# Tiles of a two-layer hybrid backbone at other SBUF addresses, with the order of all work kept

## The chip, the cores and the metric

The kernel runs on one core of one Trainium2 chip. The metric is device time in microseconds of one execution; the times shown are single executions and their median.

## What is computed

The reference is a backbone of two layers over 256 context and 256 latent tokens of width 1024. Each layer is a SwiGLU FFN, a token mixer and a second SwiGLU FFN, each after an RMSNorm with a shift, a scale and a gate made from the conditioning vectors. The mixer of layer 0 is a state-space scan (S5), that of layer 1 a gated DeltaNet.

```python
def swiglu(h, w13, w2):
    a, b = jnp.split(h @ w13, 2, axis=-1)
    return (jax.nn.silu(a) * b) @ w2
...
for i in range(DEPTH):
    mx = (silu(c) @ mod_w[i] + mod_b[i]).reshape(bsz, N_MOD, 1, D_MODEL)
    x = x + 0.5 * mx[:, 2] * swiglu(ada_norm(x, norm_g[i, 0], mx[:, 0], mx[:, 1]), ffn_w13[i, 0], ffn_w2[i, 0])
...
    hx = ada_norm(x, norm_g[i, 1], mx[:, 3], mx[:, 4])
...
    x = x + mx[:, 5] * ox
    x = x + 0.5 * mx[:, 8] * swiglu(ada_norm(x, norm_g[i, 2], mx[:, 6], mx[:, 7]), ffn_w13[i, 1], ffn_w2[i, 1])
return rms_norm(x, final_g)
```

## The kernel before

**Layout and stages.** Activations lie with the channel on the partitions: x is 8 tiles of 128 partitions x 512 tokens in float32. The program runs straight through: the modulation vectors, norm, FFN 0, norm, S5 and its gated linear unit, norm, FFN 1, norm, FFN 2, norm, DeltaNet and its output projection, norm, FFN 3, final norm. FFN 3 and the output projection work on the 256 latent tokens alone. An FFN goes over its 22 inner tiles in three parts of 8, 8 and 6; each part has an up phase and a down phase.

**Matmuls of three.** Every large matrix product is done as three float32r matmuls: weights and activations are both split into a high and a low part, and high x high, high x low and low x high are added in PSUM. `mm3` (lines 219 to 221) does this for one output tile, `mm3_pair` (line 228) for two. The activation parts are hh and hl in the up phases, the GLU and the DeltaNet projections, hidh and hidl in the down phases, and yh and yl in the output projection. The weight parts are whi and wlo.

**Weights.** A block is 1 MB of weights in one of two slots of raw. SyncE loads it in two halves (`load_halves`, line 237), ScalarE copies each half to whi (`split_hi`, line 254), VectorE subtracts to get wlo (`split_lo`, line 260), and TensorE reads 48 weight tiles of 128 x 128 from a full block. Each step waits on a semaphore of its half and slot.

**Other lines that are spoken of.** ScalarE's SiLU (line 495) and VectorE's product (line 522) fill gt; GpSimd makes hidh (line 573) and hidl (line 575) from it; VectorE adds the down projection to x (line 558). A norm squares x on GpSimd (line 348), takes the reciprocal on VectorE (line 366), scales x into tmp (line 373) and makes hh (line 324) and hl (line 384). Line 592 has the modulation matmuls, which read cvec, and line 1430 writes gwal, at the beginning of the DeltaNet stage.

**Queues and order.** The order of each engine's work is written out in the program, with semaphores alone between the engines. Loads of weights go through SyncE's queue. No instruction depends on an address.

**SBUF.** Tiles are given addresses one after another in the order in which they are declared. A tile that is declared in a stack that has been closed gives its bytes back, so that later tiles lie over it; such overlays hold the FFN's tiles (hidh, hidl, modw, rows, cb, junk, gt, hh, hl), those of the S5 tables and scan, and those of the DeltaNet, each beginning at byte 99,200 of a partition. The first tile, x, begins at byte 16,512. With the sizes in the program this gives, in bytes of one partition:

| tile | bytes | begins before | past a multiple of 2048 |
|---|---|---|---|
| x | 16,384 | 16,512 | 128 |
| raw | 16,384 | 32,896 | 128 |
| whi | 16,384 | 49,280 | 128 |
| wlo | 16,384 | 65,664 | 128 |
| consts | 6,144 | 82,048 | 128 |
| mods, gs, hg | 1,920 | 88,192 | 128 |
| rstd | 2,048 | 90,336 | 224 |
| gwal | 1,024 | 97,152 | 896 |
| cvec | 1,024 | 98,176 | 1,920 |
| hidh | 16,384 | 99,200 | 896 |
| hidl | 16,384 | 115,584 | 896 |
| modw | 16,384 | 131,968 | 896 |
| gt | 4,096 | 192,384 | 1,920 |
| hh | 16,384 | 196,480 | 1,920 |
| hl | 16,384 | 212,864 | 1,920 |
| yh (DeltaNet) | 9,216 | 179,040 | 864 |

One row of hh, hidh or x for a tile of channels is 2,048 bytes (512 tokens); the latent tokens are its second 1,024 bytes. A weight tile is 512 bytes, four of them 2,048. A row of yh is 1,024 bytes.

Of the kernel before, what the change touches and what calls it, by code (L numbers as in the profile page):

```python
# [14 lines left out]
F32 = mybir.dt.float32  # L15
# [4 lines left out]
P = 128  # L20
D = 1024
KT = D // P
# [6 lines left out]
NMOD = 9  # L29
# [94 lines left out]
def program(nc, A, out):  # L124

    ctx = ExitStack()
    with ctx:
# [6 lines left out]
        def sb(name, shape, dt=F32, stack=None):  # L134
            return (stack or ctx).enter_context(nc.sbuf_tensor(name, shape, dt))


        x = sb("x", [P, KT, T])
        raw = sb("raw", [P, 2, BLK])
        whi = sb("whi", [P, 2, BLK], F32R)  # L140
        wlo = sb("wlo", [P, 2, BLK], F32R)
        consts = sb("consts", [P, len(CONSTS), P])
        mods = sb("mods", [P, 2, NMOD * KT, 2])
        gs = sb("gs", [P, 2, 3, KT, 2])
        hg = sb("hg", [P, 2, 3, KT, 2])
        ng = sb("ng", [P, 2, 3, KT])
        fg = sb("fg", [P, KT])
        rstd = sb("rstd", [P, T])
# [7 lines left out]
        early.close()  # L156
        gwa = sb("gwa", [P, KT, 4 * H])
        gwah = sb("gwah", [P, KT, 4 * H], F32R)
        gwal = sb("gwal", [P, KT, 4 * H], F32R)
        cvec = sb("cvec", [P, KT, 32])  # L160
        PS = ctx.enter_context(nc.psum_tensor("PS", [P, 8, 512], F32))

        def const(name):
# [1 line left out]


        ffn = ExitStack()
        hidh = sb("hidh", [P, PARTS[0][1], T], F32R, ffn)
        hidl = sb("hidl", [P, PARTS[0][1], T], F32R, ffn)
        modw = sb("modw", [P, MS, 4 * 512], F32, ffn)  # L170
        rows = sb("rows", [P, 512], F32, ffn)
        cb = sb("cb", [P, 2, D], F32, ffn)
# [4 lines left out]
        hl = sb("hl", [P, KT, T], F32R, ffn)  # L177
        ffn.close()
        nrm = ExitStack()
        tmp = sb("tmp", [P, KT, T], F32, nrm)  # L180
        nrm.close()

# [466 lines left out]
                    dve.tensor_scalar(hg[:, layer, n, :, :], one, 1.0 if n == 1 else 0.5, None, ALU.mult).then_inc(mods_ready, 1)  # L649

        prs = ExitStack()
        sb("hid_at", [P, 6144], F32, prs)
        ep = sb("ep", [P, 2, 6, 64], F32, prs)
        sb("ep_end", [P, 256], F32, prs)
# [16 lines left out]
        t4 = sb("t4", [P, GPB * (L + 1) * C16], F32, prs)  # L671
        prs.close()
        ups = ExitStack()
        sb("to_hh", [P, 24320], F32, ups)
        v = sb("v", [P, 24, 64], F32, ups)
        s5p = sb("s5p", [P, 3, 64], F32, ups)
# [9 lines left out]
        yd = nc.dram_tensor("yd", (D, T), F32, kind="Internal").ap()  # L686

        s5st = ExitStack()
        U = sb("U", [P, G, NK], F32, s5st)
        hS = sb("hS", [P, KT, L, NK], F32, s5st)  # L690
        vwS = sb("vwS", [P, 2, 2, 8, P], F32, s5st)
# [396 lines left out]
        def s5_sp(sp):  # L1088
# [5 lines left out]
            for part_, (k0, k1) in enumerate(S5_PARTS):  # L1094
# [5 lines left out]
                for st in range(L):  # L1100
                    src = bass.AP(hd.tensor, hd.offset + k0 * P * T + st * NK, [[T, C16], [C16 * T, 8 * (k1 - k0)], [1, NK]])
                    sp.dma_start(U[C16 * st:C16 * st + C16, 8 * k0:8 * k1, :], src).then_inc(u_in[part_], 16)
                if part_ == 0:
# [15 lines left out]
        def scan_order(t, d):  # L1119

            return t if d == 0 else t.rearrange("p (a j) -> p a j", a=2)[:, :, ::-1]

        def s5_pe(pe):
            def inputs(b):
# [5 lines left out]
                for gd in range(8):  # L1130
                    for r in range(2):
                        for g2 in range(2):
                            g = 8 * b + 2 * (gd // 2) + g2
                            last = pe.matmul(PS[64 * g2:64 * g2 + 64, 2 * s + r, gd * NK:(gd + 1) * NK],
                                             vwS[:, s, r, gd, 64 * g2:64 * g2 + 64], scan_order(U[:, g, :], gd % 2),
                                             start=True, stop=True)
                last.then_inc(V_ready, 1)

            def outputs(c):
                s = c % 2  # L1140

                def dst(pr, g2):
                    return PS[:, 4 + 2 * s + g2, pr * NK:(pr + 1) * NK]
# [5 lines left out]
                for pr in range(GPB):  # L1149
                    for g2 in range(2):  # L1150
                        gl = 2 * pr + g2
                        pe.matmul(dst(pr, g2), mS[:, s, gl, :], U[:, 8 * c + gl, :], start=pr == 0, stop=False,
                                  skip_group_check=True)
# [156 lines left out]
                    last.then_inc(blk_done[s], 1)  # L1310

        gst = ExitStack()
        pk = sb("pk", [P, 2, CTX + 4], F32, gst)
        pv = sb("pv", [P, 2, CTX + 4], F32, gst)
        pq = sb("pq", [P, 1, LAT + 4], F32, gst)
# [823 lines left out]
```

## Time and profile before

| | |
|---|---|
| three runs | 2404.7, 2392.39, 2399.65 us |
| median | 2399.65 us |
| profiled execution, its own time | 2398.18 us |
| its span, first to last instruction | 2396.4 us |
| busy share, TensorE, VectorE, ScalarE, GpSimd | 89%, 67%, 29%, 32% |
| chain that ended last: matmuls of line 228 | 36.2% of the span |
| chain that ended last: matmuls of lines 219 to 221 | 15.8% of the span |

The busy share is the part of the span in which an engine had an instruction of the program running. Matmuls overlap in the pipeline, so what one costs in a steady run is read from the distance of their starts, not from their durations. The chain that ended last is followed back from the last instruction, at each step to what released it. The granted clock is the share of TensorE's full clock: 1.00 is 2.4 GHz and 0.50 is 1.2 GHz.

### The profile page before, as it was taken

To read this page: it belongs to the slowest core of one execution; us is meant where nothing else is said; L and a number is where in the kernel's file an instruction comes from. 1 tells how busy PE (TensorE), PEld (TensorE's weight loads), DVE (VectorE), ACT (ScalarE), POOL (GpSimd) and SP (SyncE) were. 2 spreads that over 40 slices of the span, in tenths; PEclk is the share of its full clock that TensorE was granted. 3 is DMA by queue.
4 is the path that set the end of the run, shared out by engine and by line. 5 is a ranking of instruction groups with operands and counts; after the bars stand their busy time and mean duration, and the time that the engine had idled before them with its cause. 6 is when DMAs were issued, how large, how long until landed. Compare 5 with 4: busy or idle time off the path is not lost.

```text
span 2396.4 us, 34067 instructions
## 1 busy us (share of the span) xinstructions
PE 2125.8 (89%) x12486; PEld 1811.1 (76%) x12486; DVE 1609.4 (67%) x2255; ACT 704.0 (29%) x992; POOL 755.7 (32%) x588
## 2 busy tenths in 40 slices
PE   3898998972889899999899999869999999788997
PEld 0676777752878688887688888668888888778997
DVE  7966886853433886858894854637777777745555
ACT  1311221231133321212331222333434434324432
POOL 2243663742523120203320202303333322323123
PEclk6999999996679899999999999969999999988999
DMA  7354653639943344445353532210111111003553
GB/s 285 127 210 164 214 188 143 213 134 201 295 114 121 138 169 149 180 136 182 115 202 124 195 110 88 74 43 29 35 35 35 35 35 35 0 18 128 187 177 105
DMA packets 104689, 309.62 MB, mean 129 GB/s; under 512 B 27680, under 2 KB 39456, under 8 KB 95136
## 3 DMA queue, kind: packets, MB, share of 16 engines
q1 hardware_dynamic: 89392, 285.80, 35.5%
q10 hardware_dynamic: 12528, 12.33, 1.7%
q0 software_dynamic: 2688, 10.42, 1.1%
q8 instruction: 50, 0.82, 0.1%
q14 instruction: 31, 0.25, 0.0%
HBM read 280.26 MB, written 28.25 MB: 129 GB/s over the span
## 4 chain that ended last, share of the span: by engine, by line
PE 59%; issue 16%; DVE 10%; POOL 8%; DMA 2%; ACT 2%; SPq 1%; DVEq 1%; ACTq 0%; POOLq 0%
PE PS L228 36%; PE PS L219 5%; PE PS L221 5%; PE PS L220 5%; POOL EE L1883 2%; DVE wlo L260 2%; PE PS L1161 1%; POOL DTs L1873 1%; DVE t L927 1%; POOL X L1879 1%; DMA vwS<-vwd 1%; DVE bx L928 1%; PE PS L592 1%; DVE bx L926 1%; DVE rstd L366 1%
## 5 line engine op out<-in xcount | busy, mean ns | idle before, releaser
L228 PE MATMUL PS<-hh,whi 128*128 128x512 f32 (+1 forms) x1792 | 510.6, 367 | 42.9 <-DVE hl L384 32.1
L260 DVE TENSOR_TENSOR wlo<-raw,whi 128x1024 fp32r<-128x1024 f32 x328 | 488.1, 1528 | 85.7 <-ACT whi L254 82.7
L228 PE MATMUL PS<-hl,whi 128*128 128x512 f32 (+1 forms) x1792 | 506.1, 364 | 0.0
L228 PE MATMUL PS<-hh,wlo 128*128 128x512 f32 (+1 forms) x1792 | 505.3, 363 | 0.0
L254 ACT ACTIVATE whi<-raw 128x1024 fp32r<-128x1024 f32 x328 | 329.0, 1051 | 309.4 <-PE PS L221 283.2
L228 PEld LDWEIGHTS PS<-hh,whi 128*128 128x128 f32 x1792 | 323.3, 192 | 106.7 <-issue 51.4
L228 PEld LDWEIGHTS PS<-hl,whi 128*128 128x128 f32 x1792 | 325.1, 191 | 52.6
L228 PEld LDWEIGHTS PS<-hh,wlo 128*128 128x128 f32 x1792 | 324.7, 191 | 52.7
L573 POOL CAST hidh<-gt 128x512 f32 (+2 forms) x88 | 63.1, 717 | 892.4 <-DVE gt L522 892.4
L219 PE MATMUL PS<-hidh,whi 128*128 128x512 f32 (+1 forms) x704 | 262.2, 372 | 35.4 <-DVE x L558 24.2
L220 PE MATMUL PS<-hidl,whi 128*128 128x512 f32 (+1 forms) x704 | 258.9, 368 | 0.0
L221 PE MATMUL PS<-hidh,wlo 128*128 128x512 f32 (+1 forms) x704 | 258.8, 368 | 0.0
L621 DVE CUSTOM_DVE_ANT_0 junk<-modw,cb,modb 128x1024 f32<-128x1024 f32 x160 | 215.5, 1347 | 4.3
L495 ACT ACTIVATE gt<-PS 128x512 f32<-128x512 f32 (+1 forms) x88 | 47.9, 545 | 570.9 <-PE PS L228 570.8
L558 DVE SCALAR_TENSOR_TENSOR x<-PS,hg,x 128x256 f32<-128x256 f32 (+1 forms) x176 | 77.3, 478 | 188.9 <-PE PS L221 188.5
L219 PEld LDWEIGHTS PS<-hidh,whi 128*128 128x128 f32 x704 | 135.2, 192 | 62.3 <-issue 24.5
L575 POOL TENSOR_TENSOR hidl<-gt,hidh 128x512 f32 (+2 forms) x88 | 157.0, 1784 | 12.6 <-POOL hidh L573 10.8
L522 DVE TENSOR_TENSOR gt<-gt,PS 128x512 f32<-128x512 f32 (+1 forms) x88 | 54.5, 619 | 148.1 <-ACT gt L495 146.6
L221 PEld LDWEIGHTS PS<-hidh,wlo 128*128 128x128 f32 x704 | 135.1, 192 | 21.9
L220 PEld LDWEIGHTS PS<-hidl,whi 128*128 128x128 f32 x704 | 135.4, 192 | 20.7
L1872 POOL TENSOR_TENSOR DTi<-DTm,consts 128x256 f32<-128x256 f32 x16 | 17.8, 1110 | 293.3 <-ACT DTm L1665 293.3
L1680 ACT ACTIVATE BT<-PS 128x512 f32<-128x512 f32 x80 | 47.8, 597 | 152.1 <-PE PS L1560 78.4
(298 smaller groups left out, 2951.3 us busy)
## 6 DMA issues: line engine op xcount, KB each, us to landing
modw<-in_mod_w SPq DMA_DIRECT2D x72, 1024.0 KB, 4.8
raw<-in_w_gdn SPq DMA_DIRECT2D x32, 512.0 KB, 4.0
cxd<-cx POOLq DMA_DIRECT2D x16, 576.0 KB, 4.5
cxS<-cxd SPq DMA_DIRECT2D x8, 1152.0 KB, 5.9
raw<-in_w_f0p0a SPq DMA_DIRECT2D x16, 512.0 KB, 6.6
vwd<-vws ACTq DMA_DIRECT2D x16, 512.0 KB, 7.1
raw<-in_w_f0p1a SPq DMA_DIRECT2D x16, 512.0 KB, 6.5
raw<-in_w_glu SPq DMA_DIRECT2D x16, 512.0 KB, 4.0
```

What stands on the lines that cost most here:

```text
L219: pe.matmul(dst, w_h, xh, start=first, stop=False)
L220: pe.matmul(dst, w_h, xl, start=False, stop=False)
L221: return pe.matmul(dst, w_l, xh, start=False, stop=last)
L228: ended = pe.matmul(dst, of[:, slot, c:c + P], moving, start=first and part_ == 0, stop=last and part_ == 2)
L254: act.activation(whi[:, s, c], raw[:, s, c], ACT.Copy).then_inc(whi_ready[half][s], 1)
L260: dve.tensor_tensor(wlo[:, s, c], raw[:, s, c], whi[:, s, c].bitcast(F32), ALU.subtract)\
L522: dve.tensor_tensor(gt[:, s, c0:T], gt[:, s, c0:T], PS[:, 2 + s, c0:T], ALU.mult).then_inc(gt_ready[s], 1)
L558: last = dve.scalar_tensor_tensor(out=xv, in0=pv, scalar=hg[:, layer, n, bass.ds(dt, 1), w:w + 1].rearrange("p a b -> p (a b)"), in1=xv, o ...
L573: pool.tensor_copy(hidh[:, bass.ds(2 * i + s, 1), c0:T], gt[:, s:s + 1, c0:T]).then_inc(hidh_ready[s], 1)
L575: pool.tensor_tensor(hidl[:, bass.ds(2 * i + s, 1), c0:T], gt[:, s:s + 1, c0:T], hidh[:, bass.ds(2 * i + s, 1), c0:T].bitcast(F32), ALU.su ...
L621: dve.tensor_tensor_reduce(out=junk[:, :], in0=modw[:, k % MS, D * j:D * j + D], in1=cb[:, w, :], scale=1.0, scalar=modb[:, layer, a:a + 1 ...
L1883: last = pool.tensor_tensor(EE[:, d, n, :, :], NN[:, d, :, :], const(name).unsqueeze(1).to_broadcast([P, NCH, CH]), ALU.mult)
```

## The change

The tiles mods, gs and hg (1,920 bytes together) are declared ahead of x. x, raw, whi, wlo and consts begin 1,920 bytes later, and ng and all that follow keep their places. cvec is declared in a stack of its own that is closed at once, so that gwal lies over it. The FFN's tiles then begin at byte 98,176 with a margin of 128 bytes, hidh begins at 98,304 and hidl at 114,688, and 896 bytes are left after them, so that modw and the rest keep their places. The other overlays get 1,024 unused bytes ahead, which keeps every tile in them at its place. After the change x (18,432), raw (34,816), whi (51,200), wlo (67,584), consts (83,968), hidh and hidl begin at multiples of 2,048; hh, hl and gt stay 1,920 past one.

```diff
+        mods = sb("mods", [P, 2, NMOD * KT, 2])
+        gs = sb("gs", [P, 2, 3, KT, 2])
+        hg = sb("hg", [P, 2, 3, KT, 2])
         x = sb("x", [P, KT, T])
         raw = sb("raw", [P, 2, BLK])
         whi = sb("whi", [P, 2, BLK], F32R)
         wlo = sb("wlo", [P, 2, BLK], F32R)
         consts = sb("consts", [P, len(CONSTS), P])
-        mods = sb("mods", [P, 2, NMOD * KT, 2])
-        gs = sb("gs", [P, 2, 3, KT, 2])
-        hg = sb("hg", [P, 2, 3, KT, 2])
...
+        first = ExitStack()
+        cvec = sb("cvec", [P, KT, 32], F32, first)
+        first.close()
         gwal = sb("gwal", [P, KT, 4 * H], F32R)
-        cvec = sb("cvec", [P, KT, 32])
...
         ffn = ExitStack()
+        sb("margin", [P, 32], F32, ffn)
         hidh = sb("hidh", [P, PARTS[0][1], T], F32R, ffn)
         hidl = sb("hidl", [P, PARTS[0][1], T], F32R, ffn)
+        sb("hid_end", [P, 224], F32, ffn)
...
         nrm = ExitStack()
+        sb("nrm_from", [P, 256], F32, nrm)
...
         prs = ExitStack()
+        sb("prs_from", [P, 256], F32, prs)
...
         ups = ExitStack()
+        sb("ups_from", [P, 256], F32, ups)
...
         s5st = ExitStack()
+        sb("s5st_from", [P, 256], F32, s5st)
...
         gst = ExitStack()
+        sb("gst_from", [P, 256], F32, gst)
```

## Rows read from the trace of the kernel before

**Rows 1.** The page: busy us, share and instructions of each engine; costliest groups (busy, mean ns).
```profile
PE 2125.8 (89%) x12486; PEld 1811.1 (76%) x12486; DVE 1609.4 (67%) x2255; ACT 704.0 (29%) x992; POOL 755.7 (32%) x588
...
L228 PE MATMUL PS<-hh,whi 128*128 128x512 f32 (+1 forms) x1792 | 510.6, 367 | 42.9 <-DVE hl L384 32.1
...
L219 PE MATMUL PS<-hidh,whi 128*128 128x512 f32 (+1 forms) x704 | 262.2, 372 | 35.4 <-DVE x L558 24.2
```
**Rows 2.** Chain of waits over the whole span, shares by engine and line.
```profile
by line: PE PS L228 36.2%; issue 16.3%; PE PS L219 5.4%; PE PS L221 5.2%; PE PS L220 5.2%; POOL EE L1883 2.3%; DVE wlo L260 1.6%; PE PS L1161 1.2%; POOL DTs L1873 1.1%; DVE t L927 0.9%; POOL X L1879 0.9%; DMA vwS<-vwd 0.9%; DVE bx L928 0.8%
```
**Rows 3.** Chain in order of time (start us, us, what): up phases, FFN 2 and 3.
```profile
1306.12 87.04 PE PS L228 x384
...
2257.49 46.09 PE PS L228 x384
```
**Rows 4.** Timeline (start us, us, engine, line), down phase of FFN 2: first, last of 145.
```profile
1397.08 0.39 PE L219 MATMUL PS<-hidh,whi 128*128 128x512 f32 x1
...
1429.75 0.39 PE L219 MATMUL PS<-hidh,whi 128*128 128x512 f32 x1
```
**Rows 5.** Timeline, down phase of FFN 3: first and last of 97 matmuls.
```profile
2237.89 0.28 PE L219 MATMUL PS<-hidh,whi 128*128 128x256 f32 x1
...
2249.41 0.28 PE L219 MATMUL PS<-hidh,whi 128*128 128x256 f32 x1
```
**Rows 6.** Timeline, output projection: first and last of 10, and of 97 matmuls.
```profile
2149.03 0.41 PE L220 MATMUL PS<-yl,whi 128*128 128x256 f32 x1
...
2150.95 0.41 PE L220 MATMUL PS<-yl,whi 128*128 128x256 f32 x1
...
2152.82 0.28 PE L219 MATMUL PS<-yh,whi 128*128 128x256 f32 x1
...
2164.18 0.28 PE L219 MATMUL PS<-yh,whi 128*128 128x256 f32 x1
```
**Rows 7.** Stretches of the output projection: us, PE busy, granted clock, DMA share, GB/s.
```profile
2148.30:2151.00 2.70, 2.70 (x14) 0.50 0.67 208
...
2153.00:2173.00 20.00, 19.51 (x165) 1.00 0.42 136
```
**Rows 8.** Groups by line and shape: matmuls of 256 columns.
```profile
L228 PE MATMUL PS<-hh,whi 128*128 128x256 f32 x480 | 98.2, 287 | 6.7 <-DVE hl L384 4.5 <-DVE wlo L260 2.1
...
L219 PE MATMUL PS<-hidh,whi 128*128 128x256 f32 x176 | 50.3, 286 | 3.5 <-POOL hidl L575 3.2 <-DVE x L558 0.2
```
**Rows 9.** VectorE: line 260 (ns min/median/max; waiters: us, times); lines 558 and 373 by shape.
```profile
L260 DVE TENSOR_TENSOR wlo<-raw,whi x328: 1205/1227/2416, 55.2 to 2375.4; 128x1024 fp32r<-128x1024 f32 x164
...
  PEld PS L228: 4.8, 3
...
L558 DVE SCALAR_TENSOR_TENSOR x<-PS,hg,x 128x256 f32<-128x256 f32 x136 | 59.1, 478 | 145.0 <-PE PS L221 144.6
...
L373 DVE SCALAR_TENSOR_TENSOR tmp<-x,gs,rstd 128x256 f32 x79 | 34.4, 479 | 0.8 <-DVE rstd L366 0.4
```
**Rows 10.** Line 254 and its longest wait for a transfer; line 575 and who waited.
```profile
L254 ACT ACTIVATE whi<-raw x328: 1037/1052/1067, 39.8 to 2373.6; 128x1024 fp32r<-128x1024 f32 x164
...
  DMA raw<-in_w_f0p0a: 7.7, 3
...
L575 POOL TENSOR_TENSOR hidl<-gt,hidh x88: 737/2049/2148, 81.7 to 2363.9; 128x512 f32 x44, 128x512 fp32r<-128x512 f32 x22, 128x256 f32 x22
...
  PEld PS L219: 11.6, 7
```
**Rows 11.** DMA issues (KB, us to landing), FFN 3; a stretch of it with DMA share.
```profile
raw<-in_w_f3p1a SPq DMA_DIRECT2D x16, 512.0 KB, 4.0
...
2263.00:2303.00 40.00, 40.00 (x336) 1.00 0.54 182
```
**Rows 12.** Lines 592 and 1430: durations, first and last start us.
```profile
L592 PE MATMUL PS<-modw,cvec x256: 592/617/1062, 7.4 to 507.3; 128*32 128x512 f32 x128
...
L1430 DVE TENSOR_TENSOR gwal<-gwa,gwah x1: 425/425/425, 1568.0 to 1568.0; 128x256 fp32r<-128x256 f32 x1
```

## The prediction

> **What bounds the kernel now.** I read the page's busy shares first, then the chain of waits, then the steady stretches of single phases. The page [rows 1] has TensorE busy for 89% of the span, with 67% for VectorE and about 30% each for ScalarE and GpSimd in its table. The chain of waits [rows 2] puts 36.2% of the span on the matmuls of line 228 (the up projections and the first gated-DeltaNet projection) and 5.4 + 5.2 + 5.2 = 15.8% on those of lines 219 to 221 (the down projections and the output projection). So 52% of the time, 0.52 x 2396.4 = 1246 us, is TensorE streaming matmul after matmul. The rest is spread over small dependent steps, of which no line has more than 2.3%. What one matmul costs is therefore what matters, and for a change of addresses the question is whether that cost hangs on where the operands lie.
>
> **What the change does to the work.** No instruction, wait, transfer or order is added, removed or moved; 12,486 matmuls stay 12,486. Seven tiles move: x, raw, whi, wlo and consts by +1920 bytes (from 128 past a multiple of 2048 onto one), hidh and hidl by -896 bytes (from 896 past a multiple onto one). mods, gs, hg and cvec move too, but they are small operands. hh, hl, gt, tmp, modw and all tiles of the S5 and DeltaNet stages stay. So the sum is one term for each engine that reads or writes a moved tile, and each term is (number of instructions) x (change of the duration of one).
>
> **TensorE, the large term.** In the up phases the weights move and hh stays; in the down phases weights and moving tile both move. Three comparisons inside the trace say how far an address counts.
> First, the up phase of the third FFN, 512 columns, hh at 1920 past a multiple: 87.04 us for 384 matmuls, 226.7 ns each [rows 3]. Its down phase, hidh at 896 past a multiple: 144 steps from 1397.08 to 1429.75, 32.67 / 144 = 226.9 ns [rows 4]. A thousand bytes of difference in the moving tile changed nothing.
> Second, crossing a multiple of 2048. The fourth FFN reads 256 columns, the second half of each 2048-byte row. In the up phase that is bytes 896 to 1920 past a multiple, which crosses none: 46.09 / 384 = 120.0 ns [rows 3]. In the down phase it is 1920 to 2944, which crosses one: 96 steps from 2237.89 to 2249.41, 11.52 / 96 = 120.0 ns [rows 5]. Every fourth weight tile crosses one too (it begins 1664 past a multiple and is 512 bytes long), and a run of 384 matmuls has no slow fourth. So the one property that a start on a multiple of 2048 surely changes, fewer crossings, is worth nothing.
> Third, and this one speaks for an effect: the output projection reads yh, which begins 864 past a multiple, that is at 96 modulo 128, where all the other large tiles are at 0 modulo 128. Its matmuls have the same 256 columns and the same order of weights, and 96 steps from 2152.82 to 2164.18 give 11.36 / 96 = 118.3 ns [rows 6], 1.7 ns less than 120.0. Streaming 256 columns at 2.4 GHz takes 106.7 ns, so a matmul has 13.3 ns on top with all tiles at 0 modulo 128 and 11.6 ns in this one case. At the lower clock level the extra is gone: from 2149.03 to 2150.95 nine steps took 1.92 us, 213.3 ns each [rows 6], which is 256 columns at 1.2 GHz; the granted clock is 0.50 there and 1.00 in the steady part [rows 7]. An extra of some ns that depends on how two read streams lie to each other is therefore real.
> The change keeps every moved large tile at 0 modulo 128, as it was. What changes is the place modulo 256 of weights against hh (both at 128 before; weights at 0, hh at 128 after), and the absolute place. The trace has no pair of that kind in a steady run. My bounds: at best the whole extra of 13.3 ns goes, at worst it grows by as much. I take 0, because the like rows (512 against 512 and 256 against 256, with different moving tiles) agree within 0.2 ns, and the odd one differs in a property that the change leaves alone.
> The price of one ns: in the up phases 5376 matmuls (3 x 1792 [rows 1]), of which 1440 (3 x 480 [rows 8]) at 120.0 ns and 3936 at 226.7 ns would take 892 + 173 = 1065 us; the chain has 0.362 x 2396.4 = 867 us of them, 81%, so 1 ns is 4.4 us. The down phases have 3 x 704 = 2112 matmuls [rows 1], 528 (3 x 176 [rows 8]) at 120.0 and 1584 at 226.9 ns, and the output projection 192 at 118.3; together they last 445 us and have 0.158 x 2396.4 = 379 us of the chain, 85%, so for the 2112 whose operands move 1 ns is 1.8 us. The two ends, 13.3 ns either way on all of them, are 13.3 x 6.2 = 82 us either way. Half a per cent (12 us, about what a measurement of this kernel can tell from no change; the three runs shown spread over 12.3 us) needs 1.9 ns on every matmul, or 2.7 ns on those of the up phases alone.
> The Trainium skill (SBUF — State Buffer, section "SBUF: two separate sides") says that TensorE and ScalarE have ports of their own and never wait on anyone, and names no rule by address. By that the term is exactly 0; the 118.3 against 120.0 ns of the output projection does not agree with a cost that is free of addresses.
>
> **VectorE.** Line 260 (wlo from raw and whi, 328 times) has a fastest of 1205 and a median of 1227 ns [rows 9]; slower ones, up to 2416, stand beside GpSimd work. raw, whi and wlo move together, so their places to each other are kept. Bounds: 328 x 8 ns (some third of the 22 ns between fastest and median) = 2.6 us either way, and most of it lies beside matmuls, of which the longest total wait for this line is 4.8 us [rows 9]. I take 0. Lines 558 and 373 read x at another place: 478 and 479 ns for 256 elements, the one with its other operand in PSUM, the other with rstd at 224 past a multiple [rows 9], so places show no cost there. 0.
>
> **ScalarE and GpSimd.** Line 254 (whi from raw) is 1037 to 1067 ns over all 328 [rows 10], 0. On GpSimd line 575 (hidl from gt and hidh) is the one two-input operation whose operands change places to each other: 88 times, median 2049 ns, and the longest total wait for it on TensorE is 11.6 us [rows 10]. The cover of the rest is the next block's matmuls (48 x 226.7 ns = 10.9 us). If an address took 26 ns off or put them on, 88 x 26 = 2.3 us, of which the first or last of each phase alone shows: 12 phases x 26 ns = 0.3 us. 0.
>
> **Transfers.** Weight halves of 512 KB land in 4.0 us in the fourth FFN while a block of 48 matmuls lasts 48 x 0.120 = 5.8 us, and the DMA engines are at 0.54 there [rows 11]. ScalarE's longest total wait for a weight transfer is 7.7 us, in 3 waits at the start [rows 10], so the term lies between -7.7 us and +7.7 us if they vanished or doubled; I take 0, since these first loads are queued behind modw, whose place is kept. The rows of raw start 128 bytes past a multiple of 256 before and on one after; the trace has no large transfer of the second kind.
> The Trainium skill (DMA: Bandwidth & Descriptors, section "How a descriptor splits into AXI transactions") says that a descriptor that doesn't begin on a multiple of 256 bytes costs a further transaction, which for a 4096-byte row would be 17 in place of 16. By that rule weight transfers are some 3% quicker, an estimate; on the 7.7 us above that would make the sum smaller by 0.3 us. No run here shows it.
>
> **Overlays.** cvec now shares its bytes with gwal. Line 592 reads cvec last at 507 us, line 1430 writes gwal at 1568 us [rows 12], and nothing waits anew.
>
> **Sum.** 0 on every term. The profiled execution took 2398.18 us (span 2396.4); the median of the runs shown is 2399.65, 1.5 us above. I forecast 2399 us.
>
> **Rivals.**
> (a) Faster: weights and moving tile no longer meet in the same place modulo 256 in the up phases, and part of the 13.3 ns goes. For it: the output projection shows that the extra follows the places. Against it: its extra fell by 1.7 ns only, and in a property that is kept here. With half of the extra gone, 6.7 x 4.4 = 29 us, 2370 us; with all of it 2341 us; it decides from 2.7 ns on.
> (b) Slower: the new placing makes the two read streams of TensorE meet more often (weights and hidh both start on a multiple of 2048 in the down phases, weights and hh half of 256 apart in the up phases). For it: the extra hangs on places, and nothing in the trace fixes the sign of a new pair of places. Against it: no steady run of the trace has a mean above 226.9 or 120.0. At +3.3 ns (a quarter of the extra) on up and down, 3.3 x 6.2 = 20 us, 2419 us; it decides from 1.9 ns on.
> (c) Something small only: VectorE, GpSimd or the transfers gain or lose their bounds above, 2.6 + 0.3 + 7.7 = 10.6 us, so 2388 to 2410 us; this stays within half a per cent.
>
> **How the numbers follow.** No effect, with (c): 0.77. (a): 0.13. (b): 0.10. The forecast's own range is 2388 to 2411, the spread of the runs with a little of (c). The range for 8 in 10 also takes the small ends of (a), about 4 ns on the up phases (2399 - 18 = 2381), and of (b) up to 2.6 ns (2399 + 16 = 2415). Faster by over 0.5% is (a), slower by over 0.5% is (b), the rest is within.
>
> **What the changed kernel's profile would show.** If I am right: line 228 at 87.0 us for 384 matmuls of 512 columns and 46.1 us for 384 of 256, line 219 to 221 at 226.9 and 120.0 ns a step, line 260 with a median near 1227, the chain with the same shares. (a) would show as fewer us for these 384, (b) as more, first in the down phases. I am wrong if a steady run changes by more than 2 ns a matmul.

## The result, and the profile after

| | before | after |
|---|---|---|
| runs | 2392.39 to 2404.7 us | 2419.22 to 2429.6 us |
| median of four runs each | 2401.24 us | 2426.18 us |
| profiled execution (span) | 2398.18 us (2396.4) | 2426.81 us (2425.0) |

The ratio is 1.0103, 95% interval 1.0082 to 1.0124: slower by 20 to 30 us. The forecast was 2399 us, with a range of 2381 to 2415; the result lies above it. The four runs of before are the three shown ahead of the prediction and one more, of 2402.82 us. Line numbers are 5 to 9 larger after the change: L228 is now L233, L219 to L221 are L224 to L226, L260 is L265, L254 is L259, L575 is L580.

The page of the changed kernel, the lines that answer to [rows 1]:

```profile
PE 2147.7 (89%) x12486; PEld 1810.7 (75%) x12486; DVE 1611.4 (66%) x2255; ACT 703.8 (29%) x992; POOL 752.3 (31%) x588
...
L233 PE MATMUL PS<-hh,whi 128*128 128x512 f32 (+1 forms) x1792 | 517.3, 370 | 43.7 <-DVE hl L389 32.2
...
L224 PE MATMUL PS<-hidh,whi 128*128 128x512 f32 (+1 forms) x704 | 263.2, 374 | 36.3 <-DVE x L563 25.9
```

The counts are the same and TensorE is busy 21.9 us longer (2147.7 against 2125.8); the other engines are within 3.4 us. The matmuls of line 233 come in three kinds (hh with whi, hl with whi, hh with wlo). The first grew by 6.7 us (517.3 against 510.6), the other two by 6.7 and 7.0, 20.4 us together; each kind of the down phases grew by 1.0 to 1.1. Split by shape, the three kinds of 512 columns grew by 7.1, 7.2 and 7.8 us (419.5, 415.3 and 415.0 against 412.4, 408.1 and 407.2), and those of 256 columns became 0.4 to 0.8 us shorter. So most of the time is in the matmuls of 512 columns of line 233: the up phases, the gated linear unit and the DeltaNet projections.

The chain of waits of the changed kernel, shares by line and then in order of time (start us, us, what); it answers to [rows 2] and [rows 3]:

```profile
by line: PE PS L233 37.0%; issue 16.1%; PE PS L224 5.4%; PE PS L226 5.2%; PE PS L225 5.2%; POOL EE L1892 2.3%; DVE wlo L265 1.6%; PE PS L1169 1.3%; POOL DTs L1882 1.0%; DVE t L935 0.9%; POOL X L1888 0.9%; DVE bx L936 0.8%; PE PS L597 0.8%; 
...
939.04 89.59 PE PS L233 x384
1072.22 67.21 PE PS L233 x288
...
1326.96 89.59 PE PS L233 x384
1460.11 67.21 PE PS L233 x288
2286.99 45.59 PE PS L233 x384
2356.70 34.19 PE PS L233 x288
```

Divide the length of each stretch by its number of matmuls; this is the step, the distance from one start to the next. At 512 columns 89.59 / 384 and 67.21 / 288 are 233.3 ns, where 87.04 / 384 was 226.7 [rows 3]: 6.6 ns more for each matmul. At 256 columns 45.59 / 384 is 118.7 ns, where 46.09 / 384 was 120.0: 1.3 ns less. The second part of FFN 2 began at 1306.12 before [rows 3] and begins at 1326.96 now, 20.8 us later; the second part of FFN 3 began at 2257.49 and begins at 2286.99, 29.5 us later. The lag grows through the stretches that hold up phases and projections of 512 columns and stops growing in FFN 3.

The timeline of the changed kernel, down phase of FFN 2 (first and last of 152 matmuls), then down phase of FFN 3 (94) and output projection (103):

```profile
1416.62 0.40 PE L225 MATMUL PS<-hidl,whi 128*128 128x512 f32 x1
...
1450.88 0.39 PE L226 MATMUL PS<-hidh,wlo 128*128 128x512 f32 x1
...
2267.75 0.28 PE L224 MATMUL PS<-hidh,whi 128*128 128x256 f32 x1
...
2278.91 0.28 PE L224 MATMUL PS<-hidh,whi 128*128 128x256 f32 x1
...
2180.73 0.28 PE L224 MATMUL PS<-yh,whi 128*128 128x256 f32 x1
...
2192.97 0.28 PE L224 MATMUL PS<-yh,whi 128*128 128x256 f32 x1
```

Down phases are as before: 34.26 us / 151 steps = 226.9 ns, as in [rows 4], and 11.16 / 93 = 120.0 ns, as in [rows 5]. The output projection went from 118.3 [rows 6] to 12.24 / 102 = 120.0 ns. Its own tiles, yh and yl, did not move; the weights did.

Granted clock and DMA share of the same stretches, second parts of the up phases of FFN 2 and FFN 3 (us, busy of PE, PEld, DVE, ACT, POOL, granted clock, DMA share, GB/s):

```profile
1327.50:1416.00 88.50, 88.50 (x381) 71.20 (x380) 75.00 (x87) 19.04 (x23) 18.77 (x14) 1.00 0.46 166
2287.50:2332.00 44.50, 44.50 (x377) 44.50 (x376) 25.89 (x24) 17.92 (x23) 14.39 (x14) 1.00 0.56 182
```

The granted clock is 1.00, the upper of the two levels (2.4 GHz), so the longer step isn't a lower clock. VectorE, ScalarE and the transfers (rows of the changed kernel):

```profile
L265 DVE TENSOR_TENSOR wlo<-raw,whi x328: 1204/1228/2418, 55.3 to 2404.1; 128x1024 fp32r<-128x1024 f32 x164
...
L259 ACT ACTIVATE whi<-raw x328: 1036/1050/1067, 40.0 to 2402.2; 128x1024 fp32r<-128x1024 f32 x164
...
L580 POOL TENSOR_TENSOR hidl<-gt,hidh x88: 734/2058/2153, 82.8 to 2392.5; 128x512 f32 x44, 128x512 fp32r<-128x512 f32 x22, 128x256 f32 x22
...
raw<-in_w_f3p1a SPq DMA_DIRECT2D x16, 512.0 KB, 3.9
```

Medians are 1228, 1050 and 2058 ns against 1227, 1052 and 2049 [rows 9, 10], and 3.9 against 4.0 us [rows 11]. Of wlo the mean rose as well, from 1528 to 1550 ns, 7.2 us over all 328, yet its share of the chain stayed at 1.6% [rows 2].

### The profile page after: what moved, and what is told of

It is laid out like the page before. It is cut to its first block, busy times and chain, and to the rows that moved or that the text cites. A ratio compares the mean times of both kernels' runs of the same rounds, so it can differ in the third digit from the quotient of the medians.

```text
span 2425.0 us, 34067 instructions
## 1 busy us (share of the span) xinstructions
PE 2147.7 (89%) x12486; PEld 1810.7 (75%) x12486; DVE 1611.4 (66%) x2255; ACT 703.8 (29%) x992; POOL 752.3 (31%) x588
## 4 chain that ended last, share of the span: by engine, by line
PE 60%; issue 16%; DVE 10%; POOL 8%; ACT 2%; DMA 2%; SPq 2%; DVEq 0%; ACTq 0%; POOLq 0%
PE PS L233 37%; PE PS L224 5%; PE PS L226 5%; PE PS L225 5%; POOL EE L1892 2%; DVE wlo L265 2%; PE PS L1169 1%; POOL DTs L1882 1%; DVE t L935 1%; POOL X L1888 1%; DVE bx L936 1%; PE PS L597 1%; DMA vwS<-vwd 1%; DVE bx L934 1%; DVE rstd L371 1%
## 5 line engine op out<-in xcount | busy, mean ns | idle before, releaser
L233 PE MATMUL PS<-hh,whi 128*128 128x512 f32 (+1 forms) x1792 | 517.3, 370 | 43.7 <-DVE hl L389 32.2
L265 DVE TENSOR_TENSOR wlo<-raw,whi 128x1024 fp32r<-128x1024 f32 x328 | 495.3, 1550 | 90.5 <-ACT whi L259 87.4
L233 PE MATMUL PS<-hl,whi 128*128 128x512 f32 (+1 forms) x1792 | 512.8, 367 | 0.0
L233 PE MATMUL PS<-hh,wlo 128*128 128x512 f32 (+1 forms) x1792 | 512.3, 367 | 0.0
L259 ACT ACTIVATE whi<-raw 128x1024 fp32r<-128x1024 f32 x328 | 328.9, 1051 | 315.4 <-PE PS L226 286.5
L233 PEld LDWEIGHTS PS<-hh,whi 128*128 128x128 f32 x1792 | 322.1, 191 | 113.7 <-issue 50.8
L233 PEld LDWEIGHTS PS<-hl,whi 128*128 128x128 f32 x1792 | 324.2, 190 | 59.7
L233 PEld LDWEIGHTS PS<-hh,wlo 128*128 128x128 f32 x1792 | 323.9, 190 | 59.6
L224 PE MATMUL PS<-hidh,whi 128*128 128x512 f32 (+1 forms) x704 | 263.2, 374 | 36.3 <-DVE x L563 25.9
L226 PE MATMUL PS<-hidh,wlo 128*128 128x512 f32 (+1 forms) x704 | 259.9, 369 | 0.0
L224 PEld LDWEIGHTS PS<-hidh,whi 128*128 128x128 f32 x704 | 135.7, 193 | 63.3 <-issue 24.0
L580 POOL TENSOR_TENSOR hidl<-gt,hidh 128x512 f32 (+2 forms) x88 | 157.3, 1788 | 12.6 <-POOL hidh L578 10.8
L226 PEld LDWEIGHTS PS<-hidh,wlo 128*128 128x128 f32 x704 | 135.7, 193 | 22.3
L1881 POOL TENSOR_TENSOR DTi<-DTm,consts 128x256 f32<-128x256 f32 x16 | 11.8, 738 | 294.0 <-ACT DTm L1674 294.0
```

The source lines that it names most:

```text
L224: pe.matmul(dst, w_h, xh, start=first, stop=False)
L226: return pe.matmul(dst, w_l, xh, start=False, stop=last)
L233: ended = pe.matmul(dst, of[:, slot, c:c + P], moving, start=first and part_ == 0, stop=last and part_ == 2)
L259: act.activation(whi[:, s, c], raw[:, s, c], ACT.Copy).then_inc(whi_ready[half][s], 1)
L265: dve.tensor_tensor(wlo[:, s, c], raw[:, s, c], whi[:, s, c].bitcast(F32), ALU.subtract)\
L580: pool.tensor_tensor(hidl[:, bass.ds(2 * i + s, 1), c0:T], gt[:, s:s + 1, c0:T], hidh[:, bass.ds(2 * i + s, 1), c0:T].bitcast(F32), ALU.su ...
```

## The experiments

**The question.** The reading of the two traces gives a first theory, and two rivals:

1. The step of a matmul in a steady run depends on the **distance between its moving tile and its weights, modulo 256 bytes**. Before, weights, hh and hidh all lay at 128 modulo 256: distance 0 everywhere. After, weights and hidh lie at 0 and hh at 128: distance 128 in the up phases, 0 in the down phases.
2. The absolute place of the weights counts (on a multiple of 256 or 2048 or not), for some readers more than for others.
3. The traffic of other engines, whose tiles x and raw moved too, takes something from TensorE.

Each run below moves tiles only. Distances are those of moving tile minus weights modulo 256 bytes, computed from the tiles' addresses. The runs of the kernel before on the same chip had medians of 2399.46 us (10 runs, for the first four experiments), 2399.76 (one run, for the next three) and 2400.51 (11 runs, for the last two). The six kernels from "The changed kernel with hh moved back into step" to "Distances that are no multiple of 32" were run once each, and single runs of the kernel before lie up to 12 us apart; what they show is read from the steps in their traces, not from their times.

### One part of the change alone: the inner tiles

The kernel before, with only hidh, hidl and cvec (and the overlays) moved as in the change. x, raw and the weights stay: distance 0 up, 128 down.

```
...
+        sb("margin", [P, 32], F32, ffn)
         hidh = sb("hidh", [P, PARTS[0][1], T], F32R, ffn)
         hidl = sb("hidl", [P, PARTS[0][1], T], F32R, ffn)
+        sb("hid_end", [P, 224], F32, ffn)
...
```

> Only hidh and hidl (and cvec) move as in the change; x, raw, whi, wlo and consts stay where the kernel before has them. Theory 1 (the step of a run of matmuls depends on the distance of moving tile and weights modulo 256 bytes): the down phases now have a distance of 128 modulo 256 and go from 226.9 to about 233.3 ns a step at 512 columns, 1584 x 6.4 x 0.85 = 9 us, so about 2410 us; the up phases keep 226.7. Theory 2 (what counts is that the weights begin on a multiple of 256 or 2048): the weights are not moved, so 226.9 in the down phases and 2401 us. Theory 3 (the moved x and raw disturb the reads of TensorE by the traffic of the other engines): nothing of it is here, 2401 us.

Measured: 2406.76 us, ratio 1.0042, interval 1.0026 to 1.0057. That is 7.3 us by the medians and 10 by the ratio, where theory 1 had 9. Its chain, second and third part of the up phases of FFN 2, and its timeline, down phase of FFN 2 (first and last of 169 matmuls):

```profile
1312.78 87.09 PE PS L233 x384
1444.66 65.31 PE PS L233 x288
```

```profile
1400.63 0.40 PE L225 MATMUL PS<-hidl,whi 128*128 128x512 f32 x1
...
1439.83 0.40 PE L225 MATMUL PS<-hidl,whi 128*128 128x512 f32 x1
```

Up 87.09 / 384 = 226.8 ns, down 39.20 / 168 = 233.3 ns: the slow phase has changed places. The same address of hidh that is fast in the changed kernel is slow here, with the weights at their old place. Down phases at 256 columns took 118.6 ns. Putting hidh on a multiple of 2048 is thus neither good nor bad by itself; what counts is the pair.

### The other part alone: the weights

The kernel before, with mods, gs and hg declared between raw and whi, which moves whi, wlo and consts by +1920 bytes and leaves x, raw, hh and hidh where they were: distance 128 up and down, 96 in the output projection.

```
...
         raw = sb("raw", [P, 2, BLK])
-        whi = sb("whi", [P, 2, BLK], F32R)
-        wlo = sb("wlo", [P, 2, BLK], F32R)
-        consts = sb("consts", [P, len(CONSTS), P])
         mods = sb("mods", [P, 2, NMOD * KT, 2])
         gs = sb("gs", [P, 2, 3, KT, 2])
         hg = sb("hg", [P, 2, 3, KT, 2])
+        whi = sb("whi", [P, 2, BLK], F32R)
+        wlo = sb("wlo", [P, 2, BLK], F32R)
+        consts = sb("consts", [P, len(CONSTS), P])
```

> mods, gs and hg stand between raw and whi, so whi, wlo and consts move by 1920 bytes as in the change; x, raw, hidh and hidl stay. Theory 1 (distance): up phases at 233.3 ns as in the change, and down phases, now 128 modulo 256 apart, at about 233 too: 25 + 9 us, about 2435 us. Theory 2 (place of the weights): up phases at 233.3, down phases as in the changed kernel at 226.9, 2426 us. Theory 3 (x and raw): neither moved, so 226.7 and 2401 us.

Measured: 2424.33 us, ratio 1.0118, interval 1.0091 to 1.0145. Chain, up phase of FFN 2, and timeline, down phase of FFN 2 (169 matmuls):

```profile
1321.29 89.23 PE PS L228 x384
1455.15 66.94 PE PS L228 x288
```

```profile
1410.84 0.39 PE L221 MATMUL PS<-hidh,wlo 128*128 128x512 f32 x1
...
1449.88 0.40 PE L221 MATMUL PS<-hidh,wlo 128*128 128x512 f32 x1
```

Both phases are slow, 89.23 / 384 and 39.04 / 168 = 232.4 ns; both kinds of 256 columns take 118.7 ns, and the output projection 120.0 ns. The down phases of the changed kernel have their weights at this same place and run at 226.9 ns, so theory 2 is excluded. The total is 11 us less than theory 1 had said: its steps were 5.7 ns longer and not 6.6, and the matmuls of 256 columns gave something back. With the steps as measured, 5.7 ns x (3936 + 1584) less 1.3 ns x (1440 + 528) is 28.9 us. The ratio gives 0.0118 x 2399.5 = 28.3 us, with an interval of 22 to 35, and the medians differ by 24.9 us.

### The changed kernel with hh moved back into step

The changed kernel, with tiles hh and hl of their own for FFN 1 and FFN 3 at distance 0 (on a multiple of 2048), and for FFN 2 at distance 128 but at another absolute place.

```
+        UP_AT = [0, 0, 128, 0]
...
+            sb(f"a{f_}", [P, (163840 - 98176 + UP_AT[f_]) // 4], F32, own)
+            hhs.append(sb(f"hh{f_}", [P, KT, T], F32R, own))
...
+            hh, hl = hhs[f], hls[f]
```

> The changed kernel, with own copies of hh and hl for FFN 1, 2 and 3 in free bytes. Those of FFN 1 and 3 begin on multiples of 2048 (distance 0 to the weights modulo 256), those of FFN 2 128 bytes past one (distance 128, as in the changed kernel, at another place). Theory 1: up phase of FFN 1 back at 226.7 ns, FFN 2 stays at 233.3, FFN 3 a constant 120.0; 1056 x 6.6 = 7 us less than the changed kernel, about 2419 us. Theory 2: all stay as in the changed kernel, 233.3 ns and 2426 us. Theory 3: the same as theory 2.

Measured: 2419.13 us, one run. Chain: second part of FFN 1, of FFN 2 and of FFN 3, up.

```profile
935.39 87.04 PE PS L243 x384
...
1318.79 89.59 PE PS L243 x384
...
2278.42 46.09 PE PS L243 x384
```

FFN 1 is back at 87.04 us, 226.7 ns, to the digit what such a part took in the kernel before [rows 3]; FFN 2 is at 233.3 ns; FFN 3 is at 120.0, all as theory 1 had it. x, raw, the weights and the inner tiles all lie as in the changed kernel. Theory 3 falls with this row: moving hh alone undoes the cost.

### What the cost is as a function of the distance

Each of the next kernels tries up to six further pairs at once. It is the kernel before with tiles of their own for FFN 1, 2 and 3; cvec and the overlays lie as in the change, and the rest of the code is as it was. The edit that tells them apart is the list of distances (entries for FFN 0 to 3; FFN 0 keeps the old tiles). The first has

```
+        UP_AT, DOWN_AT = [0, 128, 64, 128], [0, 64, 128, 128]
```

> The kernel before with own copies of hh, hl, hidh and hidl for FFN 1, 2 and 3 at chosen distances to the weights modulo 256: up phases 128, 64, 128, down phases 64, 128, 128. The weights stay 128 past a multiple of 2048. Theory 1: up phase of FFN 1 at 233.3 ns, down phase of FFN 2 at 233.3, the two at a distance of 64 something else than 226.7, between 216 and 240 ns. Theories 2 and 3: 226.7 everywhere, 120.0 in FFN 3.

Measured: 2406.64 us. Chain, second part of FFN 2, up (distance 64), and timeline, down phase of FFN 1 (distance 64, 146 matmuls):

```profile
1314.84 87.91 PE PS L247 x384
```

```profile
1018.72 0.39 PE L239 MATMUL PS<-hidl,whi 128*128 128x512 f32 x1
...
1051.90 0.39 PE L240 MATMUL PS<-hidh,wlo 128*128 128x512 f32 x1
```

87.91 / 384 = 228.9 and 33.18 / 145 = 228.8 ns: distance 64 costs a third of what 128 does, alike for hh and for hidh, two tiles at different absolute places in different phases. At a distance of 128, the up phase of FFN 1 and the down phase of FFN 2 took 232.4 ns where 233.3 was expected, and FFN 3 took 118.7 ns at 256 columns.

```
+        UP_AT, LOW_AT, DOWN_AT = [0, 224, 192, 64], [0, 224, 192, 64], [0, 160, 96, 32]
```

> The kernel before with own copies of the activation tiles. Distances to the weights modulo 256: up phases of FFN 1, 2, 3 at 224, 192, 64; down phases at 160, 96, 32. If the step rises with the distance either way round from 0 (64 gave 228.9 ns and 128 gave 232.4 to 233.3 ns at 512 columns): 224 at about 228, 192 at 229, 160 and 96 at 231. If the direction counts, 192 and 224 differ from 64 and 32. At 256 columns between 118 and 120 ns. Theory that only the half line of 128 bytes counts: 224, 192 and 160 all like 128, at 232 to 233. Total within 2399 to 2412 us.

Measured: 2415.44 us. Chain: second part of FFN 1 (distance 224), of FFN 2 (192) and of FFN 3 (64, 256 columns).

```profile
931.07 89.61 PE PS L247 x384
...
1321.47 89.59 PE PS L247 x384
...
2276.90 45.24 PE PS L247 x384
```

224 and 192 cost 233.3 ns both; 160 and 96 in the down phases 234.3 and 233.4 ns. A cost that grows with the distance, which I had thought of after the run before, is wrong: 64 is a dip, and a distance of 224 is as dear as 192. The time also lies above the 2399 to 2412 us that were expected.

### Only one half of hh apart

For FFN 1, hh at 0 and hl at 128 in the first kernel, and the reverse in the second; FFN 2 and 3 try further distances.

```
+        UP_AT, LOW_AT, DOWN_AT = [0, 0, 32, 96], [0, 128, 32, 96], [0, 224, 32, 192]
```

> Up phase of FFN 1: hh at distance 0, hl alone at 128. Up phases of FFN 2 and 3: 32 and 96. Down phases 224, 32, 192. If what counts is the moving tile that streams against the weights that are loaded meanwhile, only the steps that stream hl (a third) become slow, so a mean of about 226.7 + 6 / 3 = 228.9 ns in FFN 1, with the slow steps at those matmuls. If what counts is something that two neighbouring matmuls share (first moving tile against the next), the slow steps stand at the changes between hh and hl. Up phase of FFN 2 at about 227.8 ns if the step rises with the distance.

```
+        UP_AT, LOW_AT, DOWN_AT = [0, 128, 96, 224], [0, 0, 96, 224], [0, 192, 160, 96]
```

> Up phase of FFN 1: hh alone at distance 128, hl at 0: two thirds of the steps stream hh, so a mean of about 226.7 + 6 x 2 / 3 = 230.9 ns. Up phases of FFN 2 and 3: 96 and 224, the second like the output projection of the kernel before, 118.3 ns at 256 columns. Down phases 192, 160, 96: 229, 231 ns and, at 256 columns, 120.0 as in the output projection of the changed kernel (distance 96).

Measured: 2416.23 and 2422.62 us. Chain of the first, second part of FFN 1, and its timeline, down phase of FFN 3 (distance 192, 97 matmuls of 256 columns); then the chain of the second, second part of FFN 1:

```profile
933.52 88.32 PE PS L247 x384
```

```profile
2258.32 0.28 PE L240 MATMUL PS<-hidh,wlo 128*128 128x256 f32 x1
...
2269.20 0.28 PE L240 MATMUL PS<-hidh,wlo 128*128 128x256 f32 x1
```

```profile
935.37 89.03 PE PS L247 x384
```

With a third of the matmuls at distance 128, the mean is 88.32 / 384 = 230.0 ns, with two thirds 89.03 / 384 = 231.8 ns; in proportion to 6.6 ns they would be 228.9 and 231.1. Single steps of the first lie between 224 and 235 ns and repeat every six matmuls: of the two steps that begin at an hl matmul, one takes 235 ns and the other 224, less than the 226.7 ns of a run without any distance. Neither picture of the first expectation has that. So a matmul's step is no price of its own tile alone; it also depends on its neighbours.

The other phases answer the expectations in part. At 256 columns the values foretold for 224 and 96 came out (118.3 and 120.0 ns). At 512 columns the guesses did not: 32, 192 and 160 took 233.3, 233.3 and 234.3 ns, where 227.8, 229 and 231 were expected. The surprise is the down phase of FFN 3: 256 columns at distance 192 take 10.88 / 96 = 113.3 ns, 6.7 ns less than at distance 0. The kernel before is not at the best place there.

### Distances that are no multiple of 32

```
+        UP_AT, LOW_AT, DOWN_AT = [0, 0, 224, 192], [0, 0, 224, 192], [0, 0, 0, 160]
+        FINE = [0, 16, 16, 0]
```

> The kernel before with its own tiles for FFN 1, 2 and 3, so that the distance of the moving tiles from the weights, mod 256 bytes, is 16 (FFN 1 up), 240 (FFN 2 up), 192 (FFN 3 up) and 0, 0, 160 (down). Distances of 16 and 240 are tried for the first time; all earlier ones were multiples of 32. Theory 1a (the step depends on the distance in units of 32 bytes, so that 16 counts as 0 and 240 as 224): 226.7 ns in FFN 1 up, 233.3 ns in FFN 2 up. Theory 1b (only an exact multiple of 256 is free): 233.3 ns in both. FFN 3, 256 columns: if the 113.5 ns that its down phase showed at a distance of 192 belongs to the distance and not to the tile, its up phase now shows 113.5 ns too; if it belongs to the down phase, the up phase stays at 118 to 120 ns. Distance 160 has not been seen at 256 columns; the other distances gave 113.5 to 120.0. Time by 1a about 2399 + 1344 x 0.81 x 6.6 ns = 2406 us less some 8 us if FFN 3 up gains; by 1b about 2413 us less the same.

Measured: 2410.41 us. Chain: second part of FFN 1 (distance 16), of FFN 2 (240), second and third part of FFN 3 (192).

```profile
931.13 88.96 PE PS L249 x384
...
1319.54 89.60 PE PS L249 x384
...
2272.96 45.24 PE PS L249 x384
2341.89 32.68 PE PS L249 x288
```

Its timeline, first part of FFN 2 (distance 240; 288 matmuls lie between the starts of these two rows):

```profile
1200.42 0.64 PE L249 MATMUL PS<-hh,wlo 128*128 128x512 f32 x2
...
1268.58 0.64 PE L249 MATMUL PS<-hh,wlo 128*128 128x512 f32 x2
```

Neither theory held in full. Distance 16 costs 231.7 ns, so 16 bytes are enough to leave the free place, but not at the full price. Distance 240 costs 233.3 ns in the second part of FFN 2, yet 68.16 / 288 = 236.7 ns in its first part, with the same tiles: the dearest steady run of all. And FFN 3's up phase at 192 shows both speeds: 45.24 / 384 = 117.8 ns in its second part, 32.68 / 288 = 113.5 ns in its third, with the same tiles. Distance 160 gave 117.4 ns at 256 columns. The time, 2410.41 us, is some 5 us above what theory 1b had with the gain in FFN 3.

### A version that beats both

The kernel before with the FFN's and projections' matmuls of 512 columns left at distance 0, and those of 256 columns of FFN 3 and the output projection at 192.

```
+        UP_AT, LOW_AT, DOWN_AT = [0, 0, 0, 192], [0, 0, 0, 192], [0, 0, 0, 192]
...
+        sb("to_64", [P, 56], F32, gst)
         yh = sb("yh"
```

> The kernel before, with everything of 512 columns left at the distance 0 (226.7 ns), and the tiles that feed matmuls of 256 columns moved to a distance of 192 bytes mod 256 from the weights: FFN 3's own normed halves and inner tiles, and the two halves of the output projection. Theory 1: a step of 256 columns falls from 120.0 to 113.5 ns at full clock, as the down phase of FFN 3 showed at 192; FFN 3 has 1,584 of them in the kernel, about 0.85 of a gain there is on the path: 1584 x 6.5 ns x 0.85 = 8.8 us; the output projection, in part at full clock, gives up to 1 us. So about 2390 us against 2399.5, ratio 0.996. Theory 2 (the address itself counts and 113.5 ns belonged to the down phase alone): only FFN 3 down gains, 528 x 6.5 x 0.85 = 2.9 us, so 2396.5 us, ratio 0.999.

Measured: 2391.81 us, ratio 0.9956, interval 0.9941 to 0.9972 (six runs, 2386.25 to 2395.47). Chain, second part of FFN 2 and second and third part of FFN 3, and timeline, down phase of FFN 3 (95 matmuls) and output projection (97):

```profile
1310.20 87.04 PE PS L247 x384
...
2257.35 43.53 PE PS L247 x384
2323.89 32.65 PE PS L247 x288
```

```profile
2238.26 0.28 PE L239 MATMUL PS<-hidl,whi 128*128 128x256 f32 x1
...
2248.91 0.28 PE L240 MATMUL PS<-hidh,wlo 128*128 128x256 f32 x1
...
2158.03 0.28 PE L238 MATMUL PS<-yh,whi 128*128 128x256 f32 x1
...
2168.91 0.28 PE L238 MATMUL PS<-yh,whi 128*128 128x256 f32 x1
```

FFN 3's second part takes 43.53 us for 46.09 [rows 3], 113.4 ns a matmul; its down phase 10.65 / 94 = 113.3 ns for 120.0 [rows 5], the output projection 10.88 / 96 = 113.3 ns for 118.3 [rows 6]. Up phase, down phase and output projection agree, three different moving tiles, and FFN 2 keeps its 87.04 us. The 2390 us of theory 1 lie within the interval (2386 to 2394 us), the 2396.5 of theory 2 don't. The steps are those of one execution. The kernel of the section above, with the same distance, ran two parts of FFN 3 at 117.8 ns, so whether each execution gets the whole gain is not shown.

### The runs together

Mean step in ns of long steady runs at full clock, from all traces:

| distance modulo 256 | 0 | 16 | 32 | 64 | 96 | 128 | 160 | 192 | 224 | 240 |
|---|---|---|---|---|---|---|---|---|---|---|
| 512 columns | 226.7 | 231.7 | 233.3 | 229.0 | 233.4 | 232.4 or 233.3 | 234.3 | 233.3 | 233.3 | 233.3, in one part 236.7 |
| 256 columns | 120.0 | not tried | 116.6 | 117.8 | 120.0 | 118.7 | 117.4 | 113.3, in one run also 117.8 | 118.3 | not tried |

Where one distance was seen with several moving tiles (0, 64, 96, 128, 192, 224), the tiles agreed within 1 ns, with the exception at 192 that the table has. The exceptions at 192 and 240 are between parts of one phase, with the same tiles. Short runs of 48 projection matmuls of 256 columns at distance 128 lie between 118.5 and 120.1 ns in the changed kernel. The output projection fits without having been made for it: it lies at 224 before (118.3 ns) and at 96 in the changed kernel (120.0 ns), and FFN 3 at these distances took 118.3 and 120.0 ns. That the period is 256 and not 512 is supported by hh and hidh of the kernel before, 256 past the weights modulo 512, and hidh of the changed kernel, 0 past them, which all gave 226.7 to 226.9 ns. The weight tiles of one run lie at 512 bytes from each other, so no run could show a period above 512. Distances 0, 96 (at 256 columns) and 128 were seen with the weights at 0 and at 128 past a multiple of 256, all others with the weights at 128 alone; for those it isn't shown that the distance counts and not the place of the moving tile.

## Why the prediction was wrong

**What held.** Counts, order, VectorE, ScalarE, GpSimd, transfers and the overlays: each term was put at 0, and the medians of lines 260, 254 and 575 moved by 1, 2 and 9 ns and that of a load in FFN 3 by 0.1 us. The bound of 82 us was wide enough. The price of a ns was of the right kind: 5.7 to 6.6 ns on 3936 matmuls less 1.3 ns on 1440 is 21 to 24 us if all of it counts, the page's TensorE row has 21.9, and the measured ratio 20 to 30 us.

**The step that failed** is the one value of the large term: "I take 0, because the like rows (512 against 512 and 256 against 256, with different moving tiles) agree within 0.2 ns, and the odd one differs in a property that the change leaves alone." What the runs show in place of 0 is 5.7 to 6.6 ns on each matmul of 512 columns of line 228. The like rows agreed because every one of them had distance 0 modulo 256, up and down. They were one point read many times and not evidence that places don't count. What set the odd one, the output projection, apart was not its place modulo 128: it was the one pair with another distance (224). In the changed kernel yh still lies at the same place, and its step went from 118.3 to 120.0 ns as the weights moved. The change did alter that property, distance, for the up phases, and I had written so three sentences earlier: "weights at 0, hh at 128 after". The trace had "no pair of that kind", and with an extra that was shown to follow places, 0 had no better claim than a loss.

**The rivals.** (b) came nearest: "the new placing makes the two read streams of TensorE meet more often". The runs give its size. I had put 3.3 ns on up and down phases; it was 5.7 to 6.6 ns on those of 512 columns in the up phases, the gated linear unit and the projections, and none in the down phases, where weights and hidh moved to the same place modulo 256. "First in the down phases" was the wrong way round. That streams meet is still a picture: shown is only that the step changes with the distance of the two operands. (a), a gain from the same edit, came true where nobody gave it weight: at 256 columns distance 128 takes 1.3 ns off, in the changed kernel at most 1440 x 1.3 = 1.9 us, since most of its projections of 256 columns kept 120.0 ns. (c) was too small to be told apart.

**The sum.** The two profiled spans differ by 28.6 us, the medians by 24.9; the spans' excess of 3.7 is the scatter of single runs. Of 24.9, 21.9 are busy time of TensorE; the other 3 I can't place, and the interval of the ratio covers them. I had put only 81% of the up phases' term on the chain. The chain's part in this line grew from 0.362 x 2396.4 = 867 to 0.370 x 2425.0 = 897 us, more than TensorE's whole growth. That speaks against the discount, but doesn't settle it: 21 to 24 us without it and 17 to 20 with it lie too near each other for an interval of 20 to 30.

**The rules cited.** The Trainium skill (SBUF — State Buffer, section "SBUF: two separate sides") has it that TensorE never waits on anyone at SBUF. As far as it speaks of other engines, nothing here is against it: moving hh alone brought 87.04 us back while the weights, x and raw stayed. But the same section of the Trainium skill calls TensorE's port for weight loads a second, independent one, and by that the two reads would not hang on each other. The steps here, 226.7 or 233.3 ns by the distance of the two operands, do not bear that out, and I had let the rule stand next to the 0. The rule on descriptors in the Trainium skill (DMA: Bandwidth & Descriptors, section "How a descriptor splits into AXI transactions") was taken as making loads of raw some 3% quicker. By transactions, 16 for 17, it would be 6%; 3% is what its beats of 32 bytes give, 128 for 132, both estimates from that page of the Trainium skill. It tells the rule of bytes that are fetched, while raw is where the loads write. The medians after and before are 3.9 and 4.0 us in FFN 3 and 6.2 and 5.8 us in FFN 2, so no run here shows it.

**What stays open.** Why distance 0 is best at 512 columns and 192 at 256; why a distance of 128 runs at 232.4 ns in some phases and 233.3 in others, 240 at 236.7 and 233.3, and 192 at 117.8 and 113.5 ns in parts of one phase. The single steps follow a pattern that holds through a part and differs between them. In the changed kernel's second part of FFN 2 (mean 233.3) they alternate between 238 and 229 ns; in its first part, with the same tiles (mean 232.4), they run from 228 to 241 in a longer cycle; in the kernel before all are 226 or 227. So the distance doesn't fix the step alone, and what picks the pattern was not looked for. The lowest means, 226.7 and 113.3 ns, are 17/16 of the bare streaming, 213.3 and 106.7 ns; no address tried went below that on average. Putting hh and hl on a multiple of 2048 for the whole changed kernel wasn't tried; one run has them so in FFN 1 and 3 alone.

## What to carry to other kernels

Where a kernel streams float32r matmuls with a weight load for each, the two operands' SBUF addresses are a parameter: work out (moving - weights) modulo 256 for each steady run and try a few values, since the best one depends on the number of columns (0 for 512, 192 for 256 here, 3% and 6% of a step). Read the step of every part, since one phase can run at two speeds with the same tiles. Moving a tile for tidiness moves it against its partner; move both by the same number of bytes modulo 256, or neither. And rows that agree say nothing about a variable that all of them share: before taking "no effect" from them, ask which value of it the change brings that no row has.

## What the runs showed that was not expected

- A steady matmul step that depends on addresses: 226.7 to 236.7 ns at 512 columns and 113.3 to 120.0 ns at 256, with the granted clock at 1.00, all else equal.
- The dependence isn't monotone, has its best place at different distances for different widths, and a mere 16 bytes cost 5 ns.
- Single steps of slow runs fell to 224 ns, under the level of a run at distance 0, while others took up to 241; the steps influence each other, and two parts of a phase with the same tiles can differ by more than 3 ns a matmul.
